# A four-layer decoder trunk on one core: first loads in another order, key blocks copied by VectorE, activation tables loaded ahead, and four heads' weights loaded before their use, two of them scored beside the first gather slots

## The reference

```python
def peer_ffn(hn, w_q, subkeys, u_tab, v_tab):      # for each chunk of 128 tokens
    q = (xc @ w_q).reshape(PEER_TOKEN_CHUNK, PEER_HEADS, 2, PEER_D_HALF)
    s = jnp.einsum('thcd,hcnd->thcn', q, subkeys)          # scores of 2 x 128 keys
    s_top, i_top = lax.top_k(s, PEER_TOPK)
    ...                                                    # best 16 of the 16 x 16 sums -> idx, g
    u = u_tab[idx]
    act = jax.nn.gelu(jnp.einsum('td,thkd->thk', xc, u), approximate=False)
    v = v_tab[idx]
    return jnp.einsum('thk,thkd->td', (g * act), v)
for layer in range(DEPTH):
    h = h + mix(rms_norm(h, norm_mix[layer]))              # attention or convolution
    h = h + peer_ffn(rms_norm(h, norm_ffn[layer]), ...)
rms_norm(h, norm_final)
```

## Time and profile before

| | us |
|---|---|
| median of 3 runs (1608.71 to 1612.69) | 1609.47 |
| the profiled execution: time | 1609.41 |
| the profiled execution: span from first to last instruction | 1607.6 |
| PE busy / DVE busy / ACT busy / POOL busy | 1034.8 / 1105.3 / 597.8 / 598.1 |

### The profile page before, as it was taken

One profiled execution on the slowest core, in us unless ns is written; L12 is line 12 of the kernel. 1 busy time (PEld: TensorE's weight loads), 2 busy tenths in 40 slices (PEclk: granted clock), 3 DMA queues, 4 the chain that ended last, 5 costly groups with the idle time before them and its releaser, 6 DMA issues.

```text
span 1607.6 us, 20499 instructions
## 1 busy us (share of the span) xinstructions
PE 1034.8 (64%) x6572; PEld 510.0 (32%) x6572; DVE 1105.3 (69%) x3007; ACT 597.8 (37%) x1794; POOL 598.1 (37%) x516
## 2 busy tenths in 40 slices
PE   6987777677557667766666667657477744444443
PEld 3544442233224344332234445323234401101000
DVE  3334467777554589999774579779976677677774
ACT  2321444544223433544433443424535523332321
POOL 0002134443223444554433435434534444444441
PEclk9998885656767779756789879756689856555555
DMA  9316699999999999999999999999999999999996
GB/s 396 131 34 260 228 416 419 419 419 420 419 416 389 416 417 419 399 389 408 411 408 416 414 417 400 421 419 416 397 420 396 409 420 420 419 420 419 420 419 258
DMA packets 93708, 617.01 MB, mean 384 GB/s; under 512 B 10912, under 2 KB 15008, under 8 KB 24992
## 3 DMA queue, kind: packets, MB, share of 16 engines
q0 software_dynamic: 73728, 536.90, 81.4%
q1 hardware_dynamic: 18864, 78.39, 12.3%
q10 hardware_dynamic: 1008, 0.41, 0.1%
HBM read 614.61 MB, written 1.05 MB: 383 GB/s over the span
## 4 chain that ended last, share of the span: by engine, by line
DMA 37%; DVE 23%; PE 20%; issue 12%; ACT 6%; POOL 2%; DVEq 0%; POOLq 0%; ACTq 0%; SPq 0%
DMA ring<-table_dram,idx 31%; DVE ring L1477 9%; PE bank L497 7%; PE qpsum L497 6%; DMA head<-heads_dram 5%; PE ypsum L497 5%; DVE arena L1362 4%; ACT L920 2%; POOL ring L490 2%; PE spsum L497 1%; DMA arena<-c_out_dram 1%; ACT wts L920 1%; DVE topi L1411 1%; ACT ring L920 1%; ACT gel L920 1%
## 5 line engine op out<-in xcount | busy, mean ns | idle before, releaser
L490 POOL DMA_INDIRECT ring<-table_dram,idx x512 | 597.9, 1168 | 983.8 <-PE ypsum L497 718.8
L1477 DVE CUSTOM_DVE_ANT_0 ring<-xns,ring 128x1024 f32<-128x1024 f32 x512 | 623.0, 1222 | 334.5 <-DMA ring<-table_dram,idx 332.0
L497 PE MATMUL ypsum<-ring,wts 128*32 128x256 f32 x4096 | 431.5, 516 | 461.0 <-ACT wts L920 459.0
L920 ACT ACTIVATE gel<-dot 128x1 f32<-128x1 f32 x512 | 103.2, 202 | 763.6 <-DVE dot L1477 762.6
L497 PEld LDWEIGHTS ypsum<-ring,wts 128*32 128x32 f32 x4096 | 99.9, 126 | 714.6 <-ACT wts L920 662.6
L920 ACT ACTIVATE wts<-gident,gel 128x32 f32<-128x32 f32 x512 | 164.6, 321 | 17.0
L497 PE MATMUL qpsum<-head,hT 128*128 128x256 f32 (+1 forms) x416 | 126.8, 466 | 48.1 <-DMA head<-heads_dram 46.6
L497 PEld LDWEIGHTS qpsum<-head,hT 128*128 128x128 f32 (+1 forms) x416 | 95.1, 237 | 78.0 <-issue 39.9
L920 ACT ACT_TABLE_LOAD x84 | 107.8, 1283 | 13.1 <-PE bank L502 11.6
L1362 DVE SCALAR_TENSOR_TENSOR arena<-arena,cols 128x128 f32<-128x128 f32 x360 | 104.0, 344 | 0.7
L497 PE MATMUL bank<-hT,arena 128*128 128x128 f32 x512 | 75.0, 307 | 2.8 <-issue 2.8
(11 more groups left out here) (161 smaller groups left out, 1042.3 us busy)
## 6 DMA issues: line engine op xcount, KB each, us to landing
head<-heads_dram SPq DMA_DIRECT2D x50, 512.0 KB, 8.6
ring<-w_in_dram SPq DMA_DIRECT2D x4, 2048.0 KB, 16.9
ring<-table_dram,idx POOLq DMA_INDIRECT x512, 12.6
arena<-c_in_dram SPq DMA_DIRECT2D x4, 2048.0 KB, 21.5
arena<-heads_dram SPq DMA_DIRECT2D x7, 1152.0 KB, 25.1
arena<-c_out_dram SPq DMA_DIRECT2D x6, 1024.0 KB, 9.4
arena<-w_out_dram SPq DMA_DIRECT2D x1, 4096.0 KB, 38.9
head<-heads_dram SPq DMA_DIRECT2D x26, 128.0 KB, 7.5
```

What stands on the lines that cost most here:

```text
L490: pool.indirect_dma_start(out=row(b), out_offset=None, in_=table[:, :], in_offset=bass.IndirectOffsetOnAxis(ap=idx[R % 2][:, k:k + 1], axi ...
L497: return nc.tensor.matmul(o_, l, r, start=start, stop=stop, **kw)
L920: return nc.scalar.activation(out_, in_, func, **kw)
L1477: V.tensor_tensor_reduce(out=u, in0=xnr[G % 2], in1=u, scale=1.0, scalar=0.0, op0=ALU.mult, op1=ALU.add, accum_out=dot[:, k:k + 1]).then_i ...
```

## The change

- SP issues `ident` first, then x, then `cols`, then `w_in`; ACT keeps only the five small tables.
- The two key blocks of `turn_keys(0)` are copied by DVE; `turn_moba(0)` is copied by ACT after the second exponential, through banks of its own.
- ACT runs a one-element Exp and a one-element Gelu (`first_use`) ahead of the places where these are first needed.
- The weights of heads 0 to 3 are loaded whole into free memory (`load_first`, `load_first_keys`); `load_head` begins with head 4. Only heads 0 and 1 are scored before slot 0; heads 2 and 3 are at slots 0 to 4, heads 4 to 7 at slots 5, 8, 11, 14 (before: 1, 5, 9, 13). The attention of tile 1 moves by 4 to 5 slots at its start and by 4 at its end, the norm ahead of phase 1 from slot 90 to 93.
- `power` has two instructions a step where it serves one column, and `mean_square` has one instruction less.

```diff
-PAIR_SLOT = [22 + 7 * q for q in range(PAIRS)]
+PAIR_SLOT = [26 + 7 * q for q in range(PAIRS)]
-NORM_SLOT = [90, 95, 95]
+NORM_SLOT = [93, 95, 95]
-    return 1 + 4 * (h - QUAD)
+    return 5 + 3 * (h - QUAD)
...
         def _(sp):
+            sp.dma_start(ident[:, :], const_in[:, K_ID:K_ID + P]).then_inc(ident_in, 16)
             sp.dma_start(xt(0), x_in[0:P, :]).then_inc(x_loaded[0], 16)
+            sp.dma_start(cols[:, :], cols_in[:, :]).then_inc(ident_in, 16)
...
             def load_head(H):
-                layer, h = H // (TILES * HEADS), head_no(H)
-                if H:
-                    sp.wait_ge(head_taken, H)
+                layer, h, m = H // (TILES * HEADS), head_no(H), H - QUAD
+                before = H - 1 if m else H - 2
+                if m:
+                    sp.wait_ge(head_taken, m)
                 else:
-                    full(sp, EARLY_Q)
+                    full(sp, q_job(before))
...
-            for H in range(HEADS + 1):
+            full(sp, MOBA_AT[0] + 1)
+            for i in range(3):
+                load_first(0, i)
+            full(sp, HEAD_AT[0] + 3 * (ATTN_HEADS - 1) + 2)
+            for i in range(2):
+                load_first(1, i)
+            full(sp, OUT_AT + KD - 1)
+            load_first(0, 3)
+            for H in range(2):
+                load_first_keys(H)
+            full(sp, EARLY_Q)
+            for i in range(2, 4):
+                load_first(1, i)
+            for i in range(4):
+                load_first(2, i)
+            full(sp, EARLY_S)
+            for H in (2, 3):
+                load_first_keys(H)
+            full(sp, q_job(0))
+            for i in range(4):
+                load_first(3, i)
+            for H in range(QUAD, HEADS + 1):
                 load_head(H)
...
             def beside_attention(s):                       # PE
+                if s == 0:
+                    head_queries(2)
+                    head_scores(1)
+                if s == 1:
+                    head_turn(2)
+                    head_queries(3)
+                if s == 2:
+                    head_scores(2)
+                    head_turn(3)
+                if s == 3:
+                    head_scores(3)
...
-            for h in range(QUAD):
-                head_queries(h)
-                if h:
-                    head_scores(h - 1)
-                head_turn(h)
-            head_scores(QUAD - 1)
+            head_queries(0)
+            head_turn(0)
+            head_queries(1)
+            head_scores(0)
+            head_turn(1)
...
+            def first_use(func):                           # ACT
+                own.then(run(warm[:, :], ident[:, 0:1], func))
...
             run(trig[:, :], trig[:, :], ACT.Sin).then_inc(id_ready, 1)
+            first_use(ACT.Exp)
...
-            turn_keys(0)
-            turn_moba(0)
             for a in range(ATTN_HEADS):
                 exponentials(0, a)
+                if a == 1:
+                    turn_moba(0)
...
             project(1, 3)
+            first_use(ACT.Gelu)
...
-            def power(var, w, y, tmp):                     # DVE
+            def power(big, w, y, tmp):
...
-                for _ in range(3):
-                    own.then(V.scalar_tensor_tensor(out=tmp, in0=y, scalar=-0.5, in1=y, op0=ALU.mult, op1=ALU.mult))
-                    own.then(V.tensor_tensor(tmp, tmp, var, ALU.mult))
-                    own.then(V.scalar_tensor_tensor(out=y, in0=tmp, scalar=1.5, in1=y, op0=ALU.add, op1=ALU.mult))
+                for three in (3.0, 12.0, 768.0):
+                    for i in range(w):
+                        own.did(V.scalar_tensor_tensor(out=tmp[:, i:i + 1], in0=y[:, i:i + 1], scalar=big[:, i:i + 1], in1=y[:, i:i + 1],
+                                                       op0=ALU.mult, op1=ALU.mult))
+                    own.wait()
+                    own.then(V.scalar_tensor_tensor(out=y, in0=tmp, scalar=-three, in1=y, op0=ALU.add, op1=ALU.mult))
...
+            def turn_keys(t):
+                for i in range(2):
+                    j = MIX_AT[t] + J_KT + i
+                    full(dve, j)
+                    free(j, V.tensor_copy(kT[0:QK, 4 * i:4 * i + 4, t * P:(t + 1) * P],
+                                          banks[bank_no(j)][0:QK, :].rearrange("p (h t) -> p h t", h=4)))
```

More of the change, by code:

```diff
@@ L296, in build @@
                    [ring[:, RING * 2 * D + i * W2:RING * 2 * D + (i + 1) * W2] for i in range(KD // 2)]]
+        o_, pp_, left = part["o"], part["pp"], proj[0]
+        first_q = [[left[:, 0:W2], left[:, W2:2 * W2], left[:, 2 * W2:3 * W2], o_[:, 0:W2]],
+                   [pp_[:, 0:W2], pp_[:, W2:2 * W2], part["qT"][:, 0:W2], part["qT"][:, W2:2 * W2]], early_q[0]]
+        first_q.append(first_q[0])
+        first_keys = [o_[:, W2:W2 + 2 * KEYS], o_[:, W2 + 2 * KEYS:W2 + 4 * KEYS], head[:, HEAD_K:HEAD_W], vmla[1][:, 0:2 * KEYS]]
         early_keys = [head[:, HEAD_K:HEAD_W], gident[:, 0:2 * KEYS], proj[1][:, 3 * CHUNK:3 * CHUNK + 2 * KEYS],
@@ L312, in build @@
         early_in = sem("early_in")
+        first_in = [sem(f"first_in{H}") for H in range(QUAD)]
         x_loaded = [sem(f"x_loaded{t}") for t in range(TILES)]
@@ L590, in turn_moba @@
             def turn_moba(t):
-                for j, off in ((J_MQT, OFF_MQ), (J_MKT, OFF_MK)):
-                    transposes(MIX_AT[t] + j, [proj[t][:, off + i * P:off + (i + 1) * P] for i in range(4)])
+                for i, off in enumerate((OFF_MQ, OFF_MK)):
+                    transposes(MOBA_AT[t] + i, [proj[t][:, off + b * P:off + (b + 1) * P] for b in range(4)])
             def scores(t, a):
-                j, W = MIX_AT[t] + J_HEAD + 3 * a, (t + 1) * P
+                j, W = HEAD_AT[t] + 3 * a, (t + 1) * P
                 if a == 0:
-                    for i in range(MIX_AT[t] + J_QT, MIX_AT[t] + J_HEAD):
+                    for i in range(MIX_AT[t] + J_QT, MIX_AT[t] + J_MQT):
                         emptied(pe, i)
+                if a == HEADS:
+                    emptied(pe, MOBA_AT[t])
+                    emptied(pe, MOBA_AT[t] + 1)
                 bank = bank_of(pe, j)
@@ L620, in scores2 @@
             def scores2(q):
-                j = MIX_AT[1] + J_HEAD + 3 * q
+                j = HEAD_AT[1] + 3 * q
                 if q == 0:
-                    for i in range(MIX_AT[1] + J_QT, MIX_AT[1] + J_HEAD):
+                    for i in range(MIX_AT[1] + J_QT, HEAD_AT[1]):
                         emptied(pe, i)
@@ L794, in head_queries @@
                 for k in range(KD):
[L795 to L796 removed]
+                    if streamed(H) and k == KD // 2:
+                        pe.wait_ge(head_b_in, (H - QUAD + 1) * 16)
                     at_ = (h - 1) * HEAD_W + k * 2 * HALF
[L798 to L800 removed]
+                    w = first_q[H][k // 2][:, k % 2 * 2 * HALF:(k % 2 + 1) * 2 * HALF] if H < QUAD else \
+                        wq_[:, k, :] if streamed(H) else kept[:, at_:at_ + 2 * HALF]
+                    last = mm(bank[:, 0:2 * HALF], xnT[:, k, :], w, k == 0, k == KD - 1)
+                    if streamed(H) and k == KD // 2 - 1:
                         last.then_inc(head_taken, 1)
@@ L1144, in beside_heads @@
                     heads_at(p * HEADS + h, s - head_slot(p, h))
-            for dst, src in ((ident[:, :], const_in[:, K_ID:K_ID + P]), (cols[:, :], cols_in[:, :])):
-                act.dma_start(dst, src).then_inc(ident_in, 16)
             for dst, src in ((posi[:, :], pos_in[:, :]), (inv[:, :], const_in[:, K_INV:K_INV + NF]), (eq[:, 0:SEQ], mask_in[:, :]),
@@ L1376, in conv_norm @@
                 own.then(V.bn_aggr(small[:, 12:14], small[:, 0:12]))
-                own.then(V.tensor_scalar(small[:, 0:1], small[:, 13:14], EPS, None, ALU.add))
+                own.then(V.tensor_scalar(small[:, 0:1], small[:, 13:14], EPS, BIG, ALU.add, ALU.mult))
                 power(small[:, 0:1], 1, small[:, 2:3], small[:, 4:5])
```

153 lines of the change are left out of this document (86 added, 67 removed).

## The result

| | before | after |
|---|---|---|
| median, us | 1609.82 (4 runs, 1608.71 to 1612.69) | 1592.41 (4 runs, 1587.23 to 1593.73) |
| profiled execution: time / span, us | 1609.41 / 1607.6 | 1592.89 / 1591.1 |

The ratio is 0.9883, 95% interval 0.9868 to 0.9899. The kernel became 17.4 us faster; the forecast was 33 us faster, and 1592.4 lies outside its range of 1564 to 1590.

The account below looks back on a forecast made before the run. From 190 us on the prediction took DMA bytes as the bound, so time is won by moving more in the first 190 us. 1609.4 - 4.3 - 1.0 - 27 - 0.8 = 1576.3, predicted 1576 us, range 1564 to 1590.

Parts of the forecast that it names:

- First loads, -4.3: Kernel start: with `ident` and `cols` on SP, PE's first product comes at 10.9 us, not 15.20; -4.3 us (-3 to -5).
- the other bound of the prediction: Kernel start: PE's first product also has to wait for `w_in`'s first 2.1 MB, which would be in at 10.5 us.
- the reading of the Trainium skill in the prediction: DMA engines alternate between queues per packet, so moving `cols` to SP brings nothing: term 0, sum 1580.6 us; chance 0.05.
- Keys and MoBA, -1.0: Before PE's first scores: four ACT copies no longer stand ahead, so scores come at 67.6, not 68.64 us; -0.3 to -1.1.
- Heads before slot 0, and the hole, -27: From 130 to 190 us: earlier head weights and slots 0 to 4 fill the DMA hole; -27 us (-17 to -30).
- I allow 2 us of holes: 40.6 MB at 170: After slot 4: DMA idles only 2 us, so 40.6 MB are moved by 170 us, where before it was 197.2.
- heads 5 to 7 add 1.2 MB in every three slots: After the first slots: these weights plus a row freed every 3 us ask for more than 420 GB/s of DMA.
- The sign that the prediction itself names: Slices of DMA under 380 GB/s between 150 and 200 us would show the forecast wrong.
- The rival of a smaller gain: Slots 0 to 4: PE at 1.2 GHz (8 us) and head 3's weights 5 us late give 1583 to 1600 us; chance 0.20.
- Slower through round 8: Change of phase: heads 9 to 11 miss round 8's route at slot 116 and gathers stop, losing 30 to 40 us; chance 0.03.
- Final norm, -0.8: Final norm: three Newton steps and `mean_square` each have one dependent instruction less, 0.19 us each; -0.8 us.

Follow-up runs that it names:

- e4_small: Kernel before with only the new first-load order, the two early table loads and shorter Newton steps; key copies and heads as before: 1606.34 us against 1610.26.
- e2_space4: Changed kernel with heads 4 to 7 at slots 2, 6, 10 and 14 instead of 5, 8, 11 and 14: 1584.10 us.
- e5_mid: Changed kernel with heads 4 to 7 at slots 3, 7, 11 and 14, only the last spacing being three: 1584.10 us.
- e6_midswap: Changed kernel with heads 4 to 7 at slots 3, 7, 11, 14 and head 1's scores ahead of head 2's queries in slot 0: 1583.55 us.
- e10_midswap_again: Changed kernel with heads 4 to 7 at slots 3, 7, 11, 14 and head 1's scores ahead of head 2's queries, measured once more: 1584.23 us.
- e7_before3: Kernel before with only a spacing of three for heads 4 to 7 (slots 1, 4, 7, 10, not 1, 5, 9, 13): 1619.36 us against 1609.92.
- e11_midswap_noload: Changed kernel, heads 4 to 7 at slots 3, 7, 11, 14, slot 0's order swapped, no weights loaded for phase 0's heads 5 to 7: 1583.66 us.

## Why the prediction was wrong

- **First loads, -4.3.** PE's first product ran at 11.64 and not at 15.20: -3.6, within the bounds. The chain of the changed kernel says what is late next, as the other bound of the prediction had it:

```profile
1.66 0.42 SPq L402
2.08 0.04 issue
2.12 9.38 DMA ring<-w_in_dram
11.50 0.14 issue
11.64 9.12 PE bank L543 x16
```

 e4_small, with neither the heads nor the key copies changed, has that product at 11.45. The wait of 9.21 us for `cols` is gone, and the first 2 MB of `w_in`, 9.38 us, is in its place. By the reading of the Trainium skill in the prediction ("DMA: Bandwidth & Descriptors", Queues, rings and completion order) nothing would have come of the move; the measured 3.6 us speak against that reading.
- **Keys and MoBA, -1.0.** First scores at 63.42 instead of 68.64, that is -5.2 with the term above, against -5.3 forecast. The latents' products ahead of them start at 52.89 and not at 57.28, so 4.4 us of it are the first loads by then, and the stretch from there to the scores is 10.53 us where it was 11.36, so 0.8 are the copies; in e4_small, without them, it is 11.37. DVE's two copies took 1.28 us and started at 61.89. Head 0's queries came at 130.28, 5.4 us earlier. In this trace both terms together are right to 0.1 us, and each to 0.2. (By 52.08 in e4_small's trace the first loads alone have won 5.2, so a single trace is not good to better than 0.8 us here.) Of the time at the end the small parts alone brought 3.9 us (e4_small).
- **Heads before slot 0, and the hole, -27.** This is the term that failed, and its last part. Slot 0's products came at 141.25 (forecast 142). DVE's route of round 1 came at 160.74, 17.7 us earlier than at 178.39, but 4.2 us later than the forecast 156.5: the 4.9 us that the prediction puts between slots 0 and 1 (147.5 to 152.4) hold head 2's queries at 3.6, head 1's scores and the products, but not ACT's copy of these scores, 1.54 us ahead of slot 1's weight, and the queries took 5.41. Still, the lead in bytes at 160 us was 31.1 us, and 29.2 at 170. What was wrong is the sentence "I allow 2 us of holes: 40.6 MB at 170", and behind it "heads 5 to 7 add 1.2 MB in every three slots": I counted the weights of these heads as bytes that fill DMA, and never asked when SP may ask for them. There were 20.0 us of holes, 18 more than allowed, and the lead fell by 15.0 between 170 and 240. The sign that the prediction itself names, slices of under 380 GB/s between 150 and 200 us, is there: 316 from 159 to 199.
- Of these, the spacing costs 8.2 to 8.9 us in medians (e2_space4, e5_mid, e6_midswap and e10_midswap_again against the changed kernel; 8.4 to 9.0 if each is first taken against the kernel before beside it), and the mirrored edit in the kernel before costs 9.4 (e7_before3). This cause is shown. How much of it is the late request and how much the shorter time for the transfer is known roughly: SP's order alone, at a spacing of three, brings 5.2. What is left, 1583.6 to 1584.2 against the forecast 1576, fits the holes of 10.1 us that remain in e10_midswap_again, where 2 were allowed. There, 4 lie between 150 and 160 us: head 3's weights land 15.6 us after the last of their requests, beside seven gathers; PE waits 4.13 us for them and does the queries in 6.37 us. The other 6 lie from 160 to 210, where DVE is busy 25.6 us of 30 and then PE 19.8 of 20. That loads are not the limit there is shown by e11_midswap_noload; which of DVE's and PE's work is, was not tried.
- **The rival of a smaller gain** (1583 to 1600) holds the result, by another mechanism than it named. It spoke of the clock in slots 0 to 4 and of head 3's weights. Head 3's were 0.50 us late, and the late ones were those of heads 6 and 7. The slow clock was there, for heads 2, 4 and 6: 5.41, 5.71 and 6.82 us at mean granted clocks of 0.68, 0.65 and 0.56, for queries that take 3.62 to 3.69 at 1.00. But it is there with the heads apart as well. Over 3.62 us a head, heads 2 to 7 took 9.2 us more here and 6.2 in e10_midswap_again, so at most 3 us of what the spacing costs go through the clock.
- **Slower through round 8** did not happen, and the change of phase lost less than before: 418 GB/s from 480 to 500 us where it was 369. Counted as holes from windows of 10 us, from 390 to 560 us, it is 2.0 us against 3.4.
- **Final norm, -0.8.** From the first instruction of the norm (1583.74) to the scaling (1586.73) it is 2.99 us, and 3.57 before (1599.71 to 1603.28): -0.6. An instruction of a step went, but the first of the two that remain takes 0.22 us and not 0.16.

## What to carry to other kernels

When a load goes through one buffer, its time is set by its request, and the request by whatever stands ahead of it in the issuing engine's list. Before counting the bytes of a load as work that fills the DMA queue, write down for each what frees its buffer and what SP still waits for ahead of it. Here a spacing of three slots in place of four put each head's scores, and with them the next request, behind the next head's queries, left each transfer a slot less, and cost 8 to 9 us of the 26 that the rest of the change brings. And an experiment that leaves loads out takes bytes and waits away together; only the same omission in a kernel that has no such waits tells the two apart.

## What had not been expected of the hardware

- With all seven gathers landed and nothing freed, the DMA engines fell to 3 GB/s for 5 us while TensorE was busy all of it.
- The first half of head 6's weights (0.5 MB), asked for at 179.51 beside queued gathers, landed 10.9 us later, the second half of head 7's, asked for at 202.05, 7.9 us later, and head 3's 1 MB 15.9 us after the last of its requests, at 135.30. In this kernel a request beside a full ring has to be made some 8 to 16 us ahead, an estimate from these three.
- After a wait of 7.77 us, 16 passes took 6.82 us instead of 3.69; the mean granted clock from 190 to 200 us is 0.67, a mix of the levels of 1.2 and 2.4 GHz. This wait of PE was paid for a second time, with 3.1 us. After waits of 0.50 and 0.65 us (heads 3 and 5) the passes took 3.69 us.
